# Split float32 transformer blocks on one core: shorter waits in the gated recurrence, a reordered front and end, and matmuls of zeros at the start

## The reference

```python
# start of block 1
h = _rmsnorm(x, g_mix)                       # x: 256 x 1024
... = split(h @ w_in)                        # xa_q first
k, v = split(_rmsnorm(mem, g_mem) @ w_mem_kv)

# block 2, each of two layers
h = x @ w_in
y_hg = _hgrn2_group(hg_q, hg_f, hg_i, ...)   # per head, chunkwise:
    b = cumsum(logf)
    A = einsum(q * exp(b_t - b_s) * tri, k)  # 8 heads
    o = A @ v + (q * exp(b)) @ state
    o = o * rsqrt(mean(o * o) + eps) * out_g
y_mla, y_mem = ...
y = concat([y_hg * silu(gate), y_mla * silu(gate), y_mem * silu(gate)])
x = _layernorm(ALPHA * x + y @ w_out, ln_g, ln_b)
```

## Time and profile before

| | us |
|---|---|
| median of 3 runs | 1074.56 (1073.23 to 1075.25) |
| profiled execution | 1073.18 |
| its span, first to last instruction | 1071.4 |
| TensorE busy in the span | 1036.6 |
| VectorE (DVE) busy | 731.2 |
| ScalarE (ACT) busy | 653.3 |
| mean granted TensorE clock | 0.989 of full |

### The profile page before, as it was taken

The page is one execution under the profiler, slowest core; times in us unless marked ns, Lnnn a source line. Parts: engine busy times, 40 slices in busy tenths (PEclk is TensorE's granted clock), DMA queues, the critical chain, the costliest instruction groups (busy, mean ns, idle before and its releaser), DMA issues.

```text
span 1071.4 us, 19081 instructions
## 1 busy us (share of the span) xinstructions
PE 1036.6 (97%) x8048; PEld 926.5 (86%) x8048; DVE 731.2 (68%) x1085; ACT 653.3 (61%) x924; POOL 13.2 (1%) x18
## 2 busy tenths in 40 slices
PE   6999999999999999999999998999999999989996
PEld 5798987888989999988999997887899999978875
DVE  4674688885656887765555768767875465788675
ACT  6766576564465655544466776557756656765582
POOL 1000000000000000000000000100000000001000
PEclk9999999999999999999999999999999999999998
DMA  8663443566547556466544424421654555233221
GB/s 310 212 211 104 139 140 129 183 215 196 179 152 238 160 186 204 162 230 185 161 140 150 156 97 138 139 80 61 217 175 145 158 170 186 82 106 137 76 105 39
DMA packets 97832, 167.52 MB, mean 156 GB/s; under 512 B 7049, under 2 KB 32531, under 8 KB 97491
## 3 DMA queue, kind: packets, MB, share of 16 engines
q1 hardware_dynamic: 95776, 159.24, 46.3%
q0 software_dynamic: 1472, 5.51, 1.5%
q10 hardware_dynamic: 498, 1.55, 0.4%
HBM read 165.23 MB, written 1.05 MB: 155 GB/s over the span
## 4 chain that ended last, share of the span: by engine, by line
PE 87%; DVE 6%; ACT 3%; DMA 2%; issue 1%; SPq 0%; DVEq 0%; ACTq 0%
PE proj L589 13%; PE proj L591 13%; PE proj L590 13%; PE proj L598 11%; PE proj L600 11%; PE proj L599 11%; DMA raw<-in_w_in 2%; DVE wlo L1508 1%; PE mix L955 1%; PE mix L912 1%; PE mix L611 1%; PE mix L913 1%; PE mix L636 1%; PE mix L619 1%; PE mix L944 1%
## 5 line engine op out<-in xcount | busy, mean ns | idle before, releaser
L1508 DVE TENSOR_TENSOR wlo<-raw,whi 128x1024 fp32r<-128x1024 f32 (+3 forms) x303 | 355.1, 1203 | 148.8 <-ACT whi L1037 147.1
L1037 ACT ACTIVATE whi<-raw 128x1024 fp32r<-128x1024 f32 (+3 forms) x303 | 305.8, 1041 | 154.0 <-PE proj L600 67.9
L589 PE MATMUL proj<-act_hi,whi 128*128 128x256 f32 x1064 | 303.7, 285 | 3.8 <-DVE X L1566 3.1
L591 PE MATMUL proj<-act_hi,wlo 128*128 128x256 f32 x1064 | 301.0, 283 | 0.1
L590 PE MATMUL proj<-act_lo,whi 128*128 128x256 f32 x1064 | 300.9, 283 | 0.0
L589 PEld LDWEIGHTS proj<-act_hi,whi 128*128 128x128 f32 x1064 | 203.1, 191 | 7.2 <-DVE X L1566 4.0
L590 PEld LDWEIGHTS proj<-act_lo,whi 128*128 128x128 f32 x1064 | 203.2, 191 | 0.8
L591 PEld LDWEIGHTS proj<-act_hi,wlo 128*128 128x128 f32 x1064 | 203.1, 191 | 0.5 <-issue 0.3
L598 PE MATMUL proj<-whi,y_hi 128*128 128x512 f32 (+1 forms) x352 | 141.0, 401 | 2.0 <-DVE y_lo L1529 2.0
L599 PE MATMUL proj<-wlo,y_hi 128*128 128x512 f32 (+1 forms) x352 | 138.1, 392 | 0.0
L600 PE MATMUL proj<-whi,y_lo 128*128 128x512 f32 (+1 forms) x352 | 137.7, 391 | 0.0
(11 more groups left out here) (353 smaller groups left out, 1222.0 us busy)
## 6 DMA issues: line engine op xcount, KB each, us to landing
raw<-in_w_in SPq DMA_DIRECT2D x144, 512.0 KB, 4.4
raw<-in_w_up SPq DMA_DIRECT2D x88, 256.0 KB, 4.2
raw<-in_w_out SPq DMA_DIRECT2D x32, 512.0 KB, 3.7
raw<-in_w_down SPq DMA_DIRECT2D x22, 512.0 KB, 5.3
raw<-in_w_mem_kv SPq DMA_DIRECT2D x8, 512.0 KB, 8.3
raw<-in_w_mem_k SPq DMA_DIRECT2D x8, 512.0 KB, 4.0
raw<-in_w_o SPq DMA_DIRECT2D x8, 512.0 KB, 3.9
raw<-in_w_mem_v SPq DMA_DIRECT2D x8, 512.0 KB, 4.2
```

The lines of the kernel that those rows point to most:

```text
L589: mm(o, wh[:, i, wc], hi[:, k0 + i, :], start=begin and j % 2 == 0, stop=False, skip_group_check=True)
L591: last = mm(o, wl[:, i, wc], hi[:, k0 + i, :], start=False, stop=end, skip_group_check=True)
L1037: fn(whi[c % SPLIT][:, 0:w], raw[c % SLOTS][:, 0:w], ACT.Copy).then_inc(s.w_hi, 1)
L1508: tt(wlo[c % SPLIT][:, 0:w], raw[c % SLOTS][:, 0:w], f32(whi[c % SPLIT][:, 0:w]), ALU.subtract).then_inc(s.w_lo, 1)
```

## The change

It has six parts.

1. A new tile `IDLE` of 256 columns is set to zero by DVE; TensorE multiplies it (`keep_clock`) five times ahead of everything else, and six times between the transposes of mem and xak. Nobody reads the result.
2. The front on ACT and DVE is reordered: half of the turned tiles of mem ahead of piece 0, half behind it; piece 2 ahead of the squares of mem; the root ahead of piece 4; the turned tiles of h ahead of the copy of xak (ACT) and of the pieces up to 8 (DVE).
3. ACT has one piece less to split ahead of `log_forget(0)` and splits it behind `latent_out(1)`.
4. DVE adds mlaout0 to X without the splits that stood ahead of it.
5. Unit 7 writes its masked products to banks 0 and 1 instead of 2 and 3, waits for nothing of unit 6, and `keep(7)` does the waiting; `outputs(2)` moves from ahead of `products(6)` to behind it.
6. In the last layer the last three pieces of hgout1 are multiplied for block 0 and then for block 1, and DVE normalises block 0 before it adds block 1.

```diff
@@ -445,6 +446,7 @@
         XN = ar(6144, NB, DM)
+        IDLE = ar(9216, SEQ)
         QK, QKV = ar(0, 16, P), ar(2048, NB, 512)
@@ -604,6 +606,29 @@
+            def project_by_block(name, L, hi, lo, begin_at, half):
+
+                ps, at, o_token = shape[L, name], number[L, name], bank(name, L)
+                for b in range(NB):
+                    tb = slice(b * P, (b + 1) * P)
+                    k0 = sum(piece_dims(loads)[0] for loads in ps[:begin_at])
+                    for n in range(begin_at, len(ps)):
+                        pe.wait_ge(s.w_lo, at[n] + 1)
+                        k, cols = piece_dims(ps[n])
+                        wh = whi[at[n] % SPLIT][:, 0:k * cols].rearrange("p (k c) -> p k c", c=cols)
+                        wl = wlo[at[n] % SPLIT][:, 0:k * cols].rearrange("p (k c) -> p k c", c=cols)
+                        o = o_token[:, b, 0:cols]
+                        for i in range(k):
+                            end = n == len(ps) - 1 and i == k - 1
+                            mm(o, hi[:, k0 + i, tb], wh[:, i, :], start=False, stop=False)
+                            mm(o, hi[:, k0 + i, tb], wl[:, i, :], start=False, stop=False)
+                            last = mm(o, lo[:, k0 + i, tb], wh[:, i, :], start=False, stop=end)
+                        if b == NB - 1:
+                            last.then_inc(s.w_used, 1)
+                        elif n == len(ps) - 1:
+                            last.then_inc(half, 1)
+                        k0 += k
+
             def turn(n, src, tile0=0):
@@ -646,6 +671,13 @@
+            def keep_clock(n):
+
+                for _ in range(n):
+                    mm(proj[1][:, 0, 0:SEQ], IDLE[:, 0:P], IDLE, start=True, stop=True)
+
+            pe.wait_ge(s.idle_ok, 1)
+            keep_clock(5)
             pe.wait_ge(s.ident_in, 16)
@@ -655,6 +687,7 @@
             turn(KT, lambda k, b: MEM[:, b, k * P:(k + 1) * P])
+            keep_clock(6)
             project("xak", None, MEM_hi, MEM_lo, ready=lambda k: pe.wait_ge(s.mem_lo, k))
@@ -928,9 +961,10 @@
                     pe.wait_ge(s.hg_z, 8 * L + u + 1)
-                    if u:
+                    low = 0 if u == UNITS - 1 else 2
+                    if 0 < u < UNITS - 1:
                         pe.wait_ge(s.hg_cp, 8 * L + u)
-                    else:
+                    elif u == 0:
                         pe.wait_ge(s.hg_ll, 4 * L + 4)
@@ -947,7 +981,7 @@
                             zk, zq = (Z[:, l % 4, hd, :],) * 2 if l < 8 else (HKT[:, h, :], HQT[:, h, :])
-                            at_bank, at = (3, P) if l == 3 else (2, (l - 4) * P) if l < 8 else (3, 0)
+                            at_bank, at = (3, P) if l == 3 else (low, (l - 4) * P) if l < 8 else (low + 1, 0)
                             at += hd * 64
@@ -995,7 +1029,7 @@
                         squares(0)
-                    if u in (3, 5, 7):
+                    if u in (3, 5):
                         outputs(u // 2 - 1)
@@ -1004,6 +1038,7 @@
                         squares(1)
+                outputs(2)
                 products(UNITS - 1)
@@ -1013,7 +1048,10 @@
                 project("hgout0", L, y_hi, y_lo, ready=y_ready, part=(3, 4))
-                project("hgout1", L, y_hi, y_lo, part=(1, 4), half=s.tok_half)
+                if L + 1 < LAYERS:
+                    project("hgout1", L, y_hi, y_lo, part=(1, 4), half=s.tok_half)
+                else:
+                    project_by_block("hgout1", L, y_hi, y_lo, 1, s.tok_half)
                 if L + 1 < LAYERS:
@@ -1116,10 +1154,11 @@
+            act.wait_ge(*stage(1, None))
+            turned("mem", None, KT // 2, MEM_hi, lambda k: cols1[:, 1, k:k + 1])
             split_until(1)
-            act.wait_ge(*stage(1, None))
-            turned("mem", None, KT, MEM_hi, lambda k: cols1[:, 1, k:k + 1])
-            split_until(2)
+            turned("mem", None, KT // 2, MEM_hi, lambda k: cols1[:, 1, k:k + 1], KT // 2)
+            split_until(SLOTS - 1)
             FIRST_SS, FIRST_R = stat[:, 232:236], stat[:, 236:240]
@@ -1130,8 +1169,8 @@
             link(last)
+            rsqrt(FIRST_R, FIRST_SS, DM, EPS, None).then_inc(s.norm_r, 1)
             split_until(SLOTS + 1)
-            rsqrt(FIRST_R, FIRST_SS, DM, EPS, None).then_inc(s.norm_r, 1)
@@ -1142,8 +1181,8 @@
+            turned("h", None, KT, act_hi, lambda k: cols1[:, 0, k:k + 1])
             leave_mem("xak", QK[:, 8:16, :].rearrange("p (b h) d -> p b (h d)", b=NB))
-            turned("h", None, KT, act_hi, lambda k: cols1[:, 0, k:k + 1])
             leave_mem("xav", QKV)
@@ -1373,7 +1412,7 @@
                 shares_turned(1)
-                split_until(ahead_of("hgi1", L, 2))
+                split_until(ahead_of("hgi1", L, 1))
@@ -1425,6 +1464,7 @@
                 latent_out(1)
+                split_until(ahead_of("hgi1", L, 2))
                 weights(0, 0, 2)
@@ -1566,6 +1606,7 @@
             link = links(dve, s.dve_chain)
+            nc.vector.memset(IDLE, 0.0).then_inc(s.idle_ok, 1)
             nc.vector.memset(epsb[:, 0:1], EPS)
@@ -1573,15 +1614,17 @@
+            turned("mem", None, KT // 2, MEM_hi, MEM_lo, lambda k: cols1[:, 1, k:k + 1], each=s.mem_lo)
             split_until(1)
-            turned("mem", None, KT, MEM_hi, MEM_lo, lambda k: cols1[:, 1, k:k + 1], each=s.mem_lo)
+            turned("mem", None, KT // 2, MEM_hi, MEM_lo, lambda k: cols1[:, 1, k:k + 1], KT // 2, s.mem_lo)
             dve.wait_ge(s.mem_lo, KT)
             nc.vector.memset(stat[:, 240:241], 0.0).then_inc(s.mixed, 1)
-            split_until(SLOTS + 1)
+            split_until(SLOTS)
             dve.wait_ge(s.x_in, 16)
             norm(0, X, 238)
+            split_until(SLOTS + 1)
+            turned("h", None, KT, act_hi, act_lo, lambda k: cols1[:, 0, k:k + 1]).then_inc(s.mixed, 1)
             split_until(pieces_until("xak", None))
-            turned("h", None, KT, act_hi, act_lo, lambda k: cols1[:, 0, k:k + 1]).then_inc(s.mixed, 1)
             split_until(pieces_until("xav", None))
@@ -1947,7 +1990,8 @@
                 logs_lower(1)
-                add_to_x("mlaout0", L)
+                dve.wait_ge(*done("mlaout0", L))
+                tt(X[:, :, 0:512], bank("mlaout0", L), X[:, :, 0:512], ALU.add).then_inc(out_of("mlaout0", L)[0], 1)
                 split_until(ahead_of("hgi1", L, 1))
@@ -1962,6 +2006,8 @@
                     dve.wait_ge(s.hg_pr, 8 * L + u + 1)
+                    if u == UNITS - 1:
+                        dve.wait_ge(s.hg_cp, 8 * L + u)
                     pair = u // 2
@@ -1977,9 +2023,10 @@
                     else:
+                        low = 0 if u == UNITS - 1 else 2
                         for l in range(4, 8):
-                            link(masked(l, mix[:, 2, (l - 4) * P:(l - 3) * P]))
-                        last = masked(8, mix[:, 3, 0:P])
+                            link(masked(l, mix[:, low, (l - 4) * P:(l - 3) * P]))
+                        last = masked(8, mix[:, low + 1, 0:P])
                     last.then_inc(s.hg_cp, 1)
@@ -2049,6 +2096,19 @@
                 add_to_x("hgout0", L)
+                def normed(b):
+
+                    r, x = stat[:, 76 + b:77 + b], X[:, b, :]
+                    dve.wait_ge(s.ln_in, 32 * L + 32)
+                    dve.wait_ge(s.ln_v, 2 * L + b + 1)
+                    dve.wait_ge(s.ln_r, 2 * L + b + 1)
+                    nc.vector.reciprocal(r, r).then_inc(s.ln_s, 1)
+                    stt(x, x, stat[:, 72 + 2 * b:73 + 2 * b], LNG, ALU.subtract, ALU.mult).then_inc(s.ln_s, 1)
+                    dve.wait_ge(s.ln_s, 4 * L + 2 * b + 2)
+                    for c in range(2):
+                        cols = slice(c * 512, (c + 1) * 512)
+                        stt(X[:, b, cols], X[:, b, cols], r, LNB[:, cols], ALU.mult, ALU.add).then_inc(s.ln_x, 1)
+
                 st = stat[:, 128:152].rearrange("p (b c s) -> p b c s", b=NB, c=2)
@@ -2073,18 +2133,11 @@
                     nc.vector.bn_aggr(stat[:, 72 + 2 * b:74 + 2 * b], st[:, b, :, :]).then_inc(s.ln_v, 1)
-                dve.wait_ge(s.ln_v, 2 * L + 2)
-                dve.wait_ge(s.ln_in, 32 * L + 32)
-                for b in range(NB):
-                    r = stat[:, 76 + b:77 + b]
-                    dve.wait_ge(s.ln_r, 2 * L + b + 1)
-                    nc.vector.reciprocal(r, r).then_inc(s.ln_s, 1)
-                    x = X[:, b, :]
-                    stt(x, x, stat[:, 72 + 2 * b:73 + 2 * b], LNG, ALU.subtract, ALU.mult).then_inc(s.ln_s, 1)
-                    dve.wait_ge(s.ln_s, 4 * L + 2 * b + 2)
-                    for c in range(2):
-                        cols = slice(c * 512, (c + 1) * 512)
-                        stt(X[:, b, cols], X[:, b, cols], r, LNB[:, cols], ALU.mult, ALU.add).then_inc(s.ln_x, 1)
+                    if L + 1 == LAYERS:
+                        normed(b)
+                if L + 1 < LAYERS:
+                    for b in range(NB):
+                        normed(b)
```

1 line of the change is left out of this document (added).

## The result

The changed kernel takes 1057.88 us (median of 4 runs, 1056.61 to 1060.81), the kernel before beside it 1074.9. The ratio is 0.985, with a 95% interval of 0.982 to 0.987: 1.5% faster, some 16 us. I had forecast 1053.2. The time lies within the range of 1049.8 to 1058.5, at its upper edge, and outside the 1051 to 1055.5 that I gave my own case.

The account below looks back on a forecast made before the run. TensorE was taken as the bound, busy 1036.6 of 1071.4 us. Gains of 3.7 + 7.1 + 3.0 + 5.8 + 1.8 = 21.4 us take 1073.18 to 1051.8, plus 1.4 for the median: 1053.2 us, range 1049.8 to 1058.5.

Parts of the forecast that it names:

- my own case: The forecast itself, 1053.2 us, with its own range of 1051 to 1055.5 us and chance 0.62.
- So I book the zeros at nothing, between -1.3 and +0.5: In the front, the eleven matmuls of zeros were to bring no net gain, between -1.3 and +0.5 us.
- The pauses come back in another place: Rival: two pauses return at half size, two half-clock stretches stay, 7.9 us missing; 1061 us, chance 0.09.
- what was to show the forecast right: Trace signs: three waits gone, parameters' transposes near 38, no busy half clock behind 10 us, 0.3 us output wait, 5.6 us end.
- the sum: All gains over the whole kernel added up: 21.4 us.
- The front: Start of kernel: reordering brings parameters' transposes 2.0 us forward and removes 1.7 of half clock, 3.7 us; pause near 28.4.
- The zeros' own steps: Front: if zeros lift the clock before 6.62, mem's transposes end at 8.6 and the six zeros at 11.2.
- The rule that I set against this: Transposes don't count as busy for the clock, so it falls back in mem's; front loses up to 1.3 us.
- First pause: First decays of each layer: earlier split logs save 2.7 us in each, plus 1.7 of half clock in the first; 7.1 us.
- Second and third pause: First gate projection's wait for the addition to X, 3.0 us; last unit's wait for masked copies, 5.8 us; both layers.
- The 0.3 us that the last outputs should wait for DVE's copies: Sign at the end of each layer: last outputs wait some 0.3 us for DVE's copies.
- The end: Last layer: normalising the first rows under TensorE's work gains 1.8 us; last matmul to last write 5.6 instead of 7.5.

Follow-up runs that it names:

- the tiny ones: Changed kernel with its eleven 128x256 matmuls of zeros replaced by eleven of 32x32; 1059.77 us, ratio 0.9852.
- the six zeros of 512 columns: Changed kernel with its eleven matmuls of zeros replaced by six of 128x512, three at each place; 1052.08 us, ratio 0.9795.
- the seven without zeros of full size: Changed kernel without zeros, the same with one of five parts undone each, and with eleven 32x32 zeros instead; 1052.97 to 1061.90 us.
- the last kernel of the table: Kernel with six 512-column zeros, ACT and DVE splitting the sixth weight piece between the halves of the tiles of h; 1051.81 us, ratio 0.9780.
- the kernel with 32 tiny ones: Changed kernel, its zeros kept, with 32 more matmuls of 32x32 zeros behind them; 1060.98 us, ratio 0.9874.
- before with zeros: Kernel before with only the eleven matmuls of zeros added; 1082.52 us, ratio 1.0089.

## Why the prediction was right and wrong

**The step that failed** is "So I book the zeros at nothing, between -1.3 and +0.5". I priced their time on TensorE and their clock. I did not price what they do to all that follows: they put 44 instructions ahead of it and so move every border between packets. That costs 4.9 us by the medians (6.8 with the tiny ones, on one chip), where the whole shortfall is 4.7. The kernel without them takes 1052.97, and my forecast was 1053.2. The row that should have led me there was in the trace of before: a stop of 0.88 us that nothing ended, in a block of small matmuls at 713.69. No rival covered it. "The pauses come back in another place" had 7.9 us missing, near the 7.2 of the stops, but 1061 us for the time and the wrong mechanism, for no margin in the units was used up. Of what was to show the forecast right, one sign failed by this: half clock with TensorE busy stands behind the stop at 965.65.

That 1052.97 and 1053.2 agree so well is in part luck. In its trace the kernel without zeros ends DVE's last write 18.7 us earlier than the kernel before, where the sum has 21.4: the front is 1.3 short and a stretch of half clock at 186 to 190 is new. The profiled execution was also 1.4 above its median. The sum is met better by the six zeros of 512 columns, which keep the front and lose the long stops: 21.1 by the trace.

**The front.** Right in size: 2.2 us at the parameters' transposes for 2.0, the pause of 1.25 at 29.34 for 1.3, and no half clock at 41.0. The zeros' own steps were right too: transposes of mem in 1.94 us for 3.65, and the last zero ends at 11.27 for 11.2.

```profile
1.19 4.63 PE L677 MATMUL proj<-arena 128*128 128x256 f32 x10 [1.19 <-DVE arena L1609]
6.74 1.94 PE L636 MATMUL mix<-const,arena 128*128 128x128 f32 x16 [0.51 <-DMA arena<-in_mem]
8.52 2.75 PE L677 MATMUL proj<-arena 128*128 128x256 f32 x12
...
23.39 0.84 PE L636 MATMUL mix<-const,arena 128*128 128x128 f32 x6 [0.78 <-DVE arena L1554]
29.34 0.50 PE L600 MATMUL proj<-whi,y_hi 128*128 128x512 f32 x1 [1.25 <-DVE wlo L1548]
```

The zeros run at half pace up to 5.8 and at full pace from 8.52, and the transposes between them at full pace. The rule that I set against this (the Trainium skill, TensorE: Matmul & The Clock Gate, Part 4) would have had the clock fall back in the transposes; this trace does not show it. That is not the whole of it: of the eight kernels whose first real matmuls follow transposes alone (before and the seven without zeros of full size), five had a stretch of 3.1 to 4.0 us at half pace within their first 5 us (0.43 us apart instead of 0.23) and three had none. So the zeros seem to bring something in the front, 0.1 to 1.5 us at the parameters' transposes (37.73 and 38.03, against 38.16 to 39.21), which I had at nothing. It is not sure: the input also lands at different times in these traces, and the last kernel of the table, with zeros as well, starts them at 38.52.

**First pause.** 2.7 + 1.7 + 2.7 predicted. At the first decays of layer 0 the gain is 6.7 for 6.4; taken alone it is worth 8.9, give or take some 4.

**Second and third pause.** In layer 0 the gain from decays to outputs is 6.6 us for 6.1; without zeros, in layer 1, 5.5 for 4.4. The 0.3 us that the last outputs should wait for DVE's copies did not come: from the end of the last products at 733.2 to the outputs at 737.03 TensorE is at work all the time, 3.8 us, just what I had given DVE.

**The end.** 5.7 us from the last matmul to the last write, for 5.6.

**What stays open.** How long a stop is. It goes from 0.2 to 3.7 us. The traces give one half of it: from the start of the packet to TensorE's next matmul it is 2.2 to 2.9 us in all thirty, so a stop is long when the packet starts late. For the shortest, of 0.21 us, it starts 2.1 us before TensorE runs out (in the last kernel of the table); for that of 2.50 us just then, at 963.1; for that of 3.71 us 1.45 later, at 687.0. What sets the packet's start is not known. The number of small matmuls between the last larger one and the border does not settle it: with 128 of them the kernel with 32 tiny ones stopped for 3.71 us, the kernel after, with 127, for 0.88, and before with zeros not at all. No trace shows when a packet is asked for. Nor is it known what decides on a stretch of half clock at 186 to 190: eight of the fourteen kernels have it, with zeros and without, on the same work.

## What to carry to other kernels

Instructions that cost no time where they stand can cost time elsewhere: whoever adds or removes instructions ahead of a dense run of small matmuls moves the point at which the engine runs out of instructions, so a wait named "issue" within such a run belongs in the sum, and the change is to be run with a few different numbers of instructions ahead. If a filler is wanted, few large matmuls in place of many small ones shift the rest by less; where the borders then fall is still to be looked at. A part whose value is to be known is best undone in a version in which the number of instructions stays the same.

## What the runs showed of the hardware

- Instructions of TensorE came in packets of 16 KB, 256 instructions. All thirty stops named "issue" lie on one grid of 256 instructions, the same in every kernel, to within three matmuls in a step and 17 in the long one.
- TensorE went on 2.2 to 2.9 us after such a packet had started, in all thirty stops. In the kernel after, the one that starts at 963.1 was followed by the matmul at 965.65, and the one at 1005.7 by 1008.07. The row of the first, from the transfers between 962.97 and 963.44 (packets, MB, share of the time of sixteen engines):

```profile
q8 instruction: 1, 0.02, 16.0%
```

- Eleven matmuls of zeros at the start made a kernel of 1074 us 8.5 us slower. The parameters' transposes started only 1.1 us later (40.96 for 39.89); two stops of 3.40 and 2.76 us and more half clock came behind.
- Half clock can come or stay away on the same work of TensorE: eight of fourteen traces have it for 3.4 us at 185 to 193 us.
